# Attention loop of two mixers: two-tile scores as two 64-row products in two banks, gates on one bank, transposes on one bank

## The reference

```python
o_a = stick_breaking_attention(...)                  # 4 heads
o_b = nsa_attention(...)                             # 8 heads: compressed + selected + window
o_c = dsa_attention(...)                             # 4 heads, keys chosen by an index score
g_a, g_b, g_c = split(sigmoid(h @ w_gate), 3)        # w_gate: 1024 x 3072
merged = g_a * (o_a @ w_br_a) + g_b * (o_b @ w_br_b) + g_c * (o_c @ w_br_c)
return merged @ w_out
```

## Time and profile before

| what | us |
|---|---|
| median of 3 runs | 2309.7 |
| the profiled execution, whole | 2308.23 |
| its span, first to last instruction | 2306.4 |
| TensorE busy | 2286.8 (99%) |
| VectorE busy | 1835.0 (80%) |
| ScalarE busy | 1151.5 (50%) |
| the attention loop, first layer of the second kind | 1368.45 to 1461.90 |
| the attention loop, second one | 1980.14 (step 1) to 2070.29 |

### The profile page before, as it was taken

The page is one execution under the profiler, slowest core; times in us unless marked ns, Lnnn a source line. Parts: engine busy times, 40 slices in busy tenths (PEclk is TensorE's granted clock), DMA queues, the critical chain, the costliest instruction groups (busy, mean ns, idle before and its releaser), DMA issues.

```text
span 2306.4 us, 42275 instructions
## 1 busy us (share of the span) xinstructions
PE 2286.8 (99%) x16096; PEld 2089.4 (91%) x16096; DVE 1835.0 (80%) x2987; ACT 1151.5 (50%) x1533; POOL 4.8 (0%) x10
## 2 busy tenths in 40 slices
PE   8999999999999999999999999999999999999999
PEld 7998999999998999999999888999999998889998
DVE  7788568778888558877878887887798788878877
ACT  5445465445444565434443676654354347656443
POOL 0000000000000000000000000000000000000000
PEclk9999999999999999999999999999999999999999
DMA  6555445555555435555556433455555554334654
GB/s 242 187 191 202 152 149 192 191 187 169 191 191 201 165 132 190 200 191 164 191 185 198 173 140 121 165 192 184 187 175 191 190 170 173 125 123 168 214 187 131
DMA packets 76383, 407.61 MB, mean 177 GB/s; under 512 B 9216, under 2 KB 9872, under 8 KB 43776
## 3 DMA queue, kind: packets, MB, share of 16 engines
q1 hardware_dynamic: 75936, 405.78, 51.6%
q0 software_dynamic: 208, 0.49, 0.1%
q10 hardware_dynamic: 144, 0.04, 0.0%
HBM read 405.23 MB, written 1.05 MB: 176 GB/s over the span
## 4 chain that ended last, share of the span: by engine, by line
PE 94%; DVE 4%; issue 1%; ACT 1%; DMA 1%; SPq 0%; DVEq 0%; ACTq 0%
PE ps_proj L571 14%; PE ps_aux L571 14%; PE ps_y L213 10%; PE ps_y L215 10%; PE ps_y L214 10%; PE ps_proj L576 7%; PE ps_aux L576 7%; PE ps_proj L213 5%; PE ps_proj L215 5%; PE ps_proj L214 5%; PE ps_y L1663 1%; PE ps_aux L1696 1%; PE ps_y L1674 1%; DVE w_lo_front L111 1%; DVE w_lo_back L111 0%
## 5 line engine op out<-in xcount | busy, mean ns | idle before, releaser
L111 DVE TENSOR_TENSOR w_lo_front<-w_raw_front,w_hi_front 128x2048 fp32r<-128x2048 f32 x242 | 553.3, 2286 | 60.3 <-ACT w_hi_front L89 58.1
L89 ACT CAST w_hi_front<-w_raw_front 128x2048 fp32r<-128x2048 f32 x242 | 462.0, 1909 | 190.7 <-PE ps_aux L571 161.1
L571 PE MATMUL ps_proj<-xt_lo_hi,w_hi_front 128*128 128x512 f32 x1408 | 511.8, 394 | 10.0 <-DVE w_lo_front L139 9.0
L571 PE MATMUL ps_aux<-xt_lo_hi,w_hi_front 128*128 128x512 f32 x1408 | 511.7, 394 | 1.1 <-DVE w_lo_front L139 1.1
L213 PE MATMUL ps_y<-hidden_lo,w_hi_back 128*128 128x256 f32 x1408 | 396.9, 282 | 0.8 <-DVE hidden_lo L761 0.3
L215 PE MATMUL ps_y<-hidden_hi,w_hi_back 128*128 128x256 f32 x1408 | 396.5, 282 | 0.0
L214 PE MATMUL ps_y<-hidden_hi,w_lo_back 128*128 128x256 f32 x1408 | 396.0, 281 | 0.0
L576 PE MATMUL ps_aux<-xt_lo_hi,w_lo_front 128*128 128x256 f32 x1408 | 371.6, 283 | 0.0
L576 PE MATMUL ps_proj<-xt_lo_hi,w_lo_front 128*128 128x256 f32 x1408 | 369.2, 282 | 0.0
L89 ACT CAST w_hi_back<-w_raw_back 128x1024 fp32r<-128x1024 f32 x252 | 265.0, 1052 | 190.6 <-PE ps_y L215 148.7
L701 ACT ACTIVATE silu_gate<-silu_gate 128x256 f32<-128x256 f32 x176 | 73.7, 419 | 493.6 <-DVE silu_gate L738 493.6
(11 more groups left out here) (395 smaller groups left out, 3703.8 us busy)
## 6 DMA issues: line engine op xcount, KB each, us to landing
w_raw_front<-in_stream SPq DMA_DIRECT2D x252, 1024.0 KB, 4.9
w_raw_back<-in_stream SPq DMA_DIRECT2D x252, 512.0 KB, 3.7
m_rel_bias<-in_rel_bias SPq DMA_DIRECT2D x2, 2048.0 KB, 8.8
m_params<-in_params SPq DMA_DIRECT2D x2, 656.0 KB, 4.3
x<-in_x SPq DMA_DIRECT2D x4, 256.0 KB, 6.1
w_raw_front<-in_stream SPq DMA_DIRECT2D x2, 512.0 KB, 6.0
out<-x SPq DMA_DIRECT2D x3, 256.0 KB, 2.2
m_dft_time<-in_dft_t POOLq DMA_DIRECT2D x1, 256.0 KB, 3.6
```

The lines of the kernel that those rows point to most:

```text
L89: self.nc.scalar.copy(self.hi[part][:, parity], self.raw[part][:, parity]).then_inc(self.hi_done[part], 1)
L111: eng.tensor_tensor(self.lo[part][:, parity], self.raw[part][:, parity], self.hi[part][:, parity].bitcast(F32), ALU.subtract).then_inc(sel ...
L571: return nc.tensor.matmul(bank[:], hi[:, cols], s.xlh[:, k].rearrange("p j t -> p (j t)"), start=k == 0, stop=k == KD - 1)
```

## The change

Two-tile scores become two products with 64 rows, 256 columns each, in two banks. Jobs in even steps use `py[0]` and `py[1]`, those in odd steps `py[3]` and `pj[1]`; one-tile jobs keep their one product, in the first bank of their pair. All gates of the loop go to `pj[0]`, so gate g waits for the copy of gate g - 1. All transposes go to `py[2]`, so those of a job wait for the copy of the job before.

```diff
+def gate_bank(s, g):
+    return s.pj[g % 2 if g < LOOP_GATE else 0][:, 0:T]
+
+def score_bank(s, job, e):
+    pair = ((s.py[0], s.py[1]), (s.py[3], s.pj[1]))[job % 2]
+    return pair[0][:, e * P:(e + 1) * P] if JOBS[job][1] == 0 else pair[e][:, 0:T]
@@ gate, TensorE
-            need("gate_ready", g - 1)
+            need("gate_ready", g - 1 if g < LOOP_GATE else g)
-        project(s, w, base, slot0, P2_GATE[g], s.pj[g % 2][:, 0:T])
+        project(s, w, base, slot0, P2_GATE[g], gate_bank(s, g))
@@ loop, TensorE
-            qc, kw = p + (NSA_HEADS // 2 if br == 3 else 0), (i + 1) * P
-            mark.inc(nc.tensor.matmul(s.py[step % 2][:, 0:2 * kw], m.qT[:, qc, i * P:(i + 1) * P],
-                                      m.kbd[:, kv, :, 0:kw]), "scores_done")
+            qc = p + (NSA_HEADS // 2 if br == 3 else 0)
+            if i == 0:
+                last = nc.tensor.matmul(s.py[0 if step % 2 == 0 else 3][:, 0:2 * P],
+                                        m.qT[:, qc, 0:P], m.kbd[:, kv, :, 0:P])
+            else:
+                for e in range(2):
+                    rows = slice(e * DH, (e + 1) * DH)
+                    last = nc.tensor.matmul(score_bank(s, step, e), m.qT[rows, qc, P:T],
+                                            m.kbd[rows, kv, e])
+            mark.inc(last, "scores_done")
-            if job >= 2:
-                need("probsT_ready", job - 1)
+            if job >= 1:
+                need("probsT_ready", job)
-                    last = nc.tensor.transpose(s.py[2 + b][:, j * P:(j + 1) * P],
+                    last = nc.tensor.transpose(s.py[2][:, j * P:(j + 1) * P],
```

More of the change, by code:

```diff
@@ L1321 @@
 LAST_JOB = {g: max(j for j in range(len(JOBS)) if job_group(j) == g) for g in range(len(GROUPS))}
-GATE_AT = dict(zip(list(range(18)) + [19, 20], range(4, GATES)))
+LOOP_GATE = 4
+GATE_AT = dict(zip(list(range(18)) + [19, 20], range(LOOP_GATE, GATES)))
 TURN_LAG, PV_LAG = 2, 3
@@ L1661, in mix2_tensor @@
             kv = {1: p // 2, 2: NSA_GROUPS + p // 2, 3: NKV - 1}[br]
-            qc, kw = p + (NSA_HEADS // 2 if br == 3 else 0), (i + 1) * P
-            mark.inc(nc.tensor.matmul(s.py[step % 2][:, 0:2 * kw], m.qT[:, qc, i * P:(i + 1) * P],
-                                      m.kbd[:, kv, :, 0:kw]), "scores_done")
+            qc = p + (NSA_HEADS // 2 if br == 3 else 0)
[8 more added lines that the diff above has]
+            mark.inc(last, "scores_done")
         if 0 <= step - TURN_LAG < len(JOBS):
             job = step - TURN_LAG
-            i, b = JOBS[job][1], job % 2
+            i = JOBS[job][1]
             need("probs_ready", job + 1)
-            if job >= 2:
-                need("probsT_ready", job - 1)
+            if job >= 1:
+                need("probsT_ready", job)
             for e in range(2):
@@ L1751, in gate @@
         chunk(P2_GATE[g])
-        mark.inc(nc.scalar.copy(m.gate[g][:, 0:T], s.pj[g % 2][:, 0:T]), "gate_ready")
+        mark.inc(nc.scalar.copy(m.gate[g][:, 0:T], gate_bank(s, g)), "gate_ready")
     def wide(b, dests):
@@ L1871, in mix2_scalar @@
             mark.inc(nc.scalar.copy(m.pT[:, b, 0:width].rearrange("p j q -> p (j q)"),
-                                    s.py[2 + b][:, 0:width * P]), "probsT_ready")
+                                    s.py[2][:, 0:width * P]), "probsT_ready")
         if step < len(JOBS):
@@ L2212, in mix2_vector @@
                 last = masked_scores(nc, m.scs[job % 3][:, at], m.nmax[:, b, e:e + 1],
-                                     s.py[b][:, at], bias, qscale[:, i, head + e:head + e + 1])
+                                     score_bank(s, job, e), bias, qscale[:, i, head + e:head + e + 1])
             mark.inc(last, "biased")
```

## The result

| | before | after |
|---|---|---|
| median of 5 runs each, us | 2309.31 (2308.62 to 2310.12) | 2321.18 (2320.52 to 2323.52) |
| profiled execution, us | 2308.23 | 2323.52 |
| its span, us | 2306.4 | 2321.7 |
| mean granted TensorE clock of the profiled execution | 1.000 | 0.998 |

The changed kernel is slower, by a ratio of 1.0053 (95% interval 1.0042 to 1.0063), + 11.9 us. Forecast: slower, + 8.8, 2318.5 in a range of 2314.5 to 2322.0.

A forecast was written before the change was run, and what follows sets the result against it. TensorE was taken to bound the loop. Gate waits less 1.21 us saved by pairs gave + 3.86 in the first layer and + 4.98 in the second; + 8.8 on 2309.7 made 2318.5 us, range 2314.5 to 2322.0.

The forecast's parts named there:

- rival 2: Pairs of scores don't run side by side, 0.86 or more each; savings go, + 11.2, 2320.9 us; chance 0.05.
- the clock case: 1.2 GHz granted behind three of six TensorE stands, 3.9 us each: + 21 in all, 2330; chance 0.07.
- The pairs: Two-tile scores in the loop: 0.63 a pair, 0.10 for entering, transposes behind 0.20; 1.21 us saved a layer.
- Rival 1: A pair of scores costs 0.43, half the full product: + 6.8, 2316.5 us; chance 0.06.
- The gates: Each loop gate waits for ScalarE's copy of the one before: first layer 2.28 + 0.25 + 0.43 + 2.11 us.
- step 3 replaces step 1: The gate wait of 2.28 in step 3 replaces the 1.98 in step 1 and isn't added to it.
- The late load: Step 10's gate copy waits for a cast, the cast for a load: 0 first layer, 1.12 us second; either can have either.
- The transposes' bank: One bank for the loop's transposes costs nothing; the nearest copy ends 1.30 us before the next transposes.
- rival 3: Clock falls to 1.2 GHz behind TensorE's stands, 3.9 us a fall; three of six give + 21, 2330; chance 0.07.
- rival 4: Gate waits don't add up since ScalarE keeps a lead, and pairs cost 0.43: - 1.1, 2308.6 us; chance 0.05.

The follow-up runs named there:

- experiment 3: Against the kernel before, only the two-tile scores become pairs of 64-row products; gates and transposes keep two banks each: 2306.96 us, ratio 0.9991, - 2.4.
- experiment 7: Pairs alone (gates and transposes on two banks each), with each pair issued twice into the same banks: 2314.24 us in one run.
- experiment 1: Against the kernel before, only the loop's gates go on one bank; scores and transposes stay as they were: 2319.99 us, ratio 1.0049, + 10.6.
- the repeated run: The changed kernel run again as it is, on one chip with the kernel that has only the gates on one bank: 2320.71 us.
- experiment 4: Changed kernel plus three unread float32 products ahead of the gates of steps 1, 3 and 20, keeping TensorE busy: 2317.21 us, ratio 1.0036, + 7.9.
- experiment 2: Against the kernel before, only the transposes go on one bank: 2309.36 us, ratio 1.0001, no change.
- the gates' edit: Against the kernel before, only the loop's gates go on one bank: 2319.99 us, and 2320.13 us when run again.

## Why the prediction was nearly right

Direction and mechanism held; the time was 2.7 us above the forecast, in the main because of the clock, which the sum had put at nothing. That it still lies under the upper end of the range, 2322.0, is luck: that end was made from rival 2 with both loads late, and the clock case was left out of it.

- **The pairs.** 0.63 forecast and measured; entering from 128 rows 0.10, measured 0.09; the transposes behind it 0.20, measured 0.19. The 1.2 us a layer are experiment 3's 2.4. Rival 1's 0.43 is what a pair costs when the one before it had the same shape (experiment 7). Its sum was off by a little: of the eight savings it names four as waited away and then keeps five, and with four it would be + 7.2. Rival 2's + 11.2 was too much: without the savings the waits of steps 9, 15 and 20 are shorter too, and the sum of the waits alone is + 10.8 (experiment 1: + 10.6). The Trainium skill (TensorEngine Tiling (Array Packing), "Theoretical Speedup" and "Key Properties") gives up to 2x for a contraction of 64 and says that a change of mode drains the engine; the runs agree with both, 0.86 to 0.43 within the shape and 0.20 for the changes; whether a drain is what the 0.20 is made of no run here shows.
- **The gates.** How much later each gate of the first layer starts than before, from the loop's first product, less the 1.5 of the clock from step 9 on, beside the forecast's sum up to there (waits less savings). The starts of before are the earlier trace rows:

| gate of step | 1 | 3 | 9 | 15 | 20 |
|---|---|---|---|---|---|
| later, us | 1.86 | 2.17 | 2.10 | 1.96 | 3.95 |
| forecast | 1.98 | 2.28 | 2.18 | 1.91 | 3.86 |

```profile
1413.36 0.38 PE L213 MATMUL ps_proj<-xn_lo_hi,w_hi_front 128*128 128x256 f32 x1
...
1441.31 0.39 PE L213 MATMUL ps_proj<-xn_lo_hi,w_hi_front 128*128 128x256 f32 x1 [0.17 <-ACT gate_store L1771]
```

  So step 1: 1374.82 - 1367.58 is 7.24, before 1372.06 - 1366.68 = 5.38. Every sum up to a gate holds within 0.12, and that step 3 replaces step 1 shows. The profile's own idle times are smaller (1.50, 1.71, 1.84), as they count from the modelled end of the last product.
- **The late load.** 1.12 stood on step 10 of the second layer. It came in step 16, with 1.44 of idle time and 1.8 in the loop, and again there in the repeated run; experiment 1 had 0.51 in step 10, experiment 4 none. "Either layer can have either" was right in kind and "step 10" was not: which load is late changes from run to run, and whichever gate meets it pays.
- **The transposes' bank.** No cost, as worked out (experiment 2).
- **The clock, rival 3.** This step failed. It had a chance of 0.07 and a price of 3.9 us a fall, against it stood that nothing in the trace showed a fall. But nothing in these loops of the trace showed a stand over 0.6 us either (0.55 in the first layer, 0.61 in the second), so the absence said little. It happened behind three of the six stands in one profile and two of them in the other, at 1.5 us each. The price was too high: I had charged gate and v products at double time throughout, where the clock was back after 3.4 us and a product took 0.21 instead of 0.12. Two to three such falls on the sum of 8.8 make + 11.8 to + 13.3; measured + 11.9 and, in the repeated run, + 11.5. Experiment 4 shows that the falls go when TensorE stands for less.
- **Not slower, rival 4.** ScalarE keeps no lead: experiment 1 costs the sum of its waits.

Left open: why the clock falls behind one stand and not behind another of the same length. In two profiles of the changed kernel it fell behind 5 of 14 stands of 1.4 to 1.9 us, in two of experiment 1 behind 0 of 12. The pairs are not needed for a fall, going by the two runs of the gates' edit with a mean clock of 0.998, and the stands of the two kernels differ in length and in time too: step 3 stands 1.69 to 1.71 us in the changed kernel and 1.54 to 1.55 in the other, step 20 1.84 to 1.85 and 1.77. That the moment at which a stand begins decides together with its length is a rival that no run here tests.

## What to carry to other kernels

Before a second buffer is given up, compare the end of its reader's last copy with the start of the next writer, step by step; the cost is that lateness, set by what is queued ahead of the copy. Where that is a long instruction on which the copy doesn't depend, the order can be turned (11.3 of 11.9 us here). A new stand on TensorE, of 1.7 us and more in these runs, can have a second price in the clock, and a trace without such stands says nothing of it. A new tile shape is cheapest beside work that doesn't use all rows and columns either: one product moved gave 1.6 us on top of the pairs' 2.4.

## What was not expected of the hardware

- Behind some stands of 1.69 to 1.85 us (and of 2.57 and 2.77) the granted clock was 0.50 for 3.4 us and the gate behind it 1.5 us longer; behind others of 1.44 to 2.77 us it stayed at 1.00.
- In the changed kernel's first profile the fall began at once in one case (2078.5, with the gate) and 1.1 and 1.4 us behind the gate's start in the two others.
- Two 64-row products side by side cost 0.43 us within the shape and 0.63 alone, and the row before them takes 0.09 to 0.10 more where it has 128 rows.
